# Four modulation chunks made into columns by TensorE, with x loaded first

## The reference, cut to what matters

```
c_act = silu(c)
mod = c_act @ w_ada + b_ada            # 1 x 6144: six vectors of 1024
sh_m, sc_m, g_m, sh_f, sc_f, g_f = split(mod, 6)
u = layer_norm(x) * (1 + sc_m) + sh_m  # mixer input
z = u @ w_in
```

## Time and profile before

| | us |
|---|---|
| median of 3 runs | 1428.12 (1427.02 to 1428.88) |
| the profiled execution, its own time | 1426.88 |
| its span in the profile | 1425.1 |
| TensorE busy in the span | 1393.0 |
| VectorE / ScalarE / GpSimd busy | 969.4 / 647.3 / 421.8 |

### The profile page before, as it was taken

How to read it: one execution, slowest core, us unless ns; L and a number is a source line. 1 busy time by engine, 2 the same in 40 slices (tenths; PEclk the granted TensorE clock), 3 DMA queues, 4 the chain that set the end, 5 groups by cost and what they waited for, 6 DMA issues and landing times.

```text
span 1425.1 us, 17299 instructions
## 1 busy us (share of the span) xinstructions
PE 1393.0 (98%) x6522; PEld 1148.6 (81%) x6522; DVE 969.4 (68%) x1340; ACT 647.3 (45%) x914; POOL 421.8 (30%) x453
## 2 busy tenths in 40 slices
PE   7799999999999999999999999999999999999996
PEld 3688888888888888888888888888888888888885
DVE  5789677776479946464768797556565646437787
ACT  5522677777542124101616774443345535343251
POOL 1006465555566000000024327333444200001315
PEclk9899999999999999999999999999999999999998
DMA  9775465654565232762622555444445878456361
GB/s 347 266 266 159 148 185 156 188 168 149 161 234 172 89 104 79 245 192 86 200 114 89 183 181 193 142 145 146 156 163 207 297 277 299 162 211 236 118 222 60
DMA packets 159083, 256.42 MB, mean 180 GB/s; under 512 B 11352, under 2 KB 81422, under 8 KB 159000
## 3 DMA queue, kind: packets, MB, share of 16 engines
q1 hardware_dynamic: 144152, 204.97, 43.1%
q0 software_dynamic: 14848, 50.34, 10.5%
HBM read 182.36 MB, written 68.71 MB: 176 GB/s over the span
## 4 chain that ended last, share of the span: by engine, by line
PE 91%; DVE 5%; ACT 2%; issue 1%; DMA 1%; SPq 0%; DVEq 0%; ACTq 0%
PE ps L2065 24%; PE ps L2067 24%; PE ps L2066 24%; PE ps L2214 11%; PE ps L2254 2%; PE ps L2264 2%; PE ps L2279 2%; PE ps L2085 1%; DVE part_lo L1922 1%; PE ps L2129 1%; PE ps L2404 1%; DVE q L1983 0%; DMA k_raw<-tw_scratch 0%; DMA ada<-in_w_ada_dram 0%; DVE w_lo L1387 0%
## 5 line engine op out<-in xcount | busy, mean ns | idle before, releaser
L2065 PE MATMUL ps<-act_hi,w_hi 128*128 128x512 f32 (+1 forms) x480 | 187.2, 390 | 9.4 <-DVE act_lo L1482 9.4
L1922 DVE TENSOR_TENSOR part_lo<-k_raw,part_hi 128x1024 fp32r<-128x1024 f32 x112 | 146.1, 1332 | 58.6 <-ACT part_hi L935 55.4
L2067 PE MATMUL ps<-act_hi,w_lo 128*128 128x512 f32 (+1 forms) x480 | 184.6, 385 | 0.0
L2066 PE MATMUL ps<-act_lo,w_hi 128*128 128x512 f32 (+1 forms) x480 | 184.6, 385 | 0.0
L2065 PE MATMUL ps<-part_hi 128*128 128x512 f32 x448 | 174.3, 389 | 0.0
L2066 PE MATMUL ps<-part_lo,part_hi 128*128 128x512 f32 x448 | 174.3, 389 | 0.0
L2067 PE MATMUL ps<-part_hi,part_lo 128*128 128x512 f32 x448 | 174.3, 389 | 0.0
L935 ACT ACTIVATE part_hi<-k_raw 128x1024 fp32r<-128x1024 f32 x112 | 116.4, 1059 | 113.6 <-DMA k_raw<-tw_scratch 48.8
L2065 PEld LDWEIGHTS ps<-act_hi,w_hi 128*128 128x128 f32 x480 | 91.1, 190 | 28.4 <-issue 5.9
L1387 DVE TENSOR_TENSOR w_lo<-w_raw,w_hi 128x1024 fp32r<-128x1024 f32 x51 | 65.9, 1291 | 65.6 <-ACT w_hi L935 65.6
L2066 PEld LDWEIGHTS ps<-act_lo,w_hi 128*128 128x128 f32 x480 | 91.2, 190 | 18.4 <-issue 1.0
(11 more groups left out here) (260 smaller groups left out, 3202.4 us busy)
## 6 DMA issues: line engine op xcount, KB each, us to landing
k_raw<-h_scratch SPq DMA_DIRECT2D x112, 256.0 KB, 4.2
w_raw<-in_w_in_dram SPq DMA_DIRECT2D x42, 512.0 KB, 4.1
ada<-in_w_ada_dram SPq DMA_DIRECT2D x8, 2048.0 KB, 9.6
tw_rows<-in_w_ff_dram POOLq DMA_DIRECT2D x64, 256.0 KB, 4.1
tw_scratch<-tw_sum POOLq DMA_DIRECT2D x32, 512.0 KB, 3.7
h_scratch<-h_sum POOLq DMA_DIRECT2D x64, 256.0 KB, 3.0
k_raw<-tw_scratch SPq DMA_DIRECT2D x64, 256.0 KB, 5.4
pair_raw<-in_w_ff_dram SPq DMA_DIRECT2D x13, 1024.0 KB, 6.3
```

Source lines behind the costliest of these rows:

```text
L1922: nc.vector.tensor_tensor(part_lo[s][:, :, :], k_raw[rs][:, :, :], f(part_hi[s][:, :, :]), ALU.subtract)\
L2065: nc.tensor.matmul(out, sh, mh, start=first, stop=False)
L2066: nc.tensor.matmul(out, sh, ml, start=False, stop=False)
L2067: return nc.tensor.matmul(out, sl, mh, start=False, stop=last)
```

## The change

x is read first, all eight tiles, then chunks 0 and 2, w_in blocks 0 and 1, chunks 1 and 3. All four mixer chunks take a new path, `direct_chunk`: a 128x128 block of the chunk is the stationary operand and c_act's single column moves past it, so that the result is a column at once. A half (four of the groups k) is 16 products, and both halves are summed by VectorE in `mixer_columns`. The row path and VectorE's work on chunks 1 and 3 go. On TensorE six transposes come first, then chunk 0 and 2 among the last two; chunks 1 and 3 are cut into eight pieces of 8 products, put between the parts of the lower stage. ScalarE's and VectorE's head loops are re-ordered tile by tile, and VectorE copies two tiles into `x_t` in place of one. Loads 3 to 6 of w_ada now wait for the chunk that held the buffer.

```diff
-N_DIRECT = 2
-ROW_ORDER = (0, 2, 1, 3)
-ADA_BANKS = {0: 0, 2: 1}
+N_DIRECT = 4
+DIRECT_ORDER = (0, 2, 1, 3)
...
             def load_ada(i):
-                if i == 3:
-                    sp.wait_ge(head_ps_done, 1)
...
+                if 3 <= i < 7:
+                    sp.wait_ge(reduced, DIRECT_ORDER.index(i - 3) + 1)
...
-            load_ada_half(0, 0)
-            load_x(range(2))
-            load_ada_half(0, 1)
-            load_x(range(2, 4))
+            load_x(range(ST))
+            load_ada(0)
...
-            load_ada_half(2, 0)
-            load_x(range(4, 6))
-            load_ada_half(2, 1)
-            load_x(range(6, ST))
+            load_ada(2)
             load_block(0)
+            load_block(1)
             load_ada(1)
-            load_block(1)
             load_ada(3)
...
-            for i in range(0, ST, 2):
...
+            for i in range(ST):
                 take_root(i, i)
+                if i >= 1:
+                    norm(i - 1, i - 1, mid[:, i - 1, :])
+                if i >= 2:
+                    save_tile(i - 2)
+            cut_hi(0)
...
+            for t in range(ST):
+                dve.wait_ge(x_in[t], 16)
+                stats(mid[:, t, :], t)
+                if t >= 1:
+                    scale_bias(t - 1, t - 1)
+            scale_bias(ST - 1, ST - 1)
...
-                link(nc.vector.tensor_tensor(out, total, bias, ALU.add))
+                link(nc.vector.tensor_tensor(out, low, bias, ALU.add))
+                link(nc.vector.tensor_tensor(out, high, out, ALU.add))
...
+            for t in (ST - 2, ST - 1):
+                dve.wait_ge(z_done, t + 1)
+                dve.wait_ge(x_copied, ST - 2)
+                nc.vector.tensor_copy(x_t[:, :, t * P:(t + 1) * P], tile_banks(t)).then_inc(x_copied, 1)
...
-            start_chunk(1)
             cut_u_lo(3)
-            end_chunk(1)
             cut_lo(2)
-            ada_chunk(3)
             mixer_columns(1)
...
+            def direct_chunk(i, half, ms=range(4)):
+
+                pe.wait_ge((ada_in, ada_end_in)[half][i % 3], 16 * (i // 3 + 1))
+                if i in (1, 3):
                     pe.wait_ge(cols_done, 1)
+                for m in ms:
+                    for k in range(4 * half, 4 * half + 4):
+                        ins = nc.tensor.matmul(ps[:, 6 + i % 2, 16 * half + 4 * i + m:16 * half + 4 * i + m + 1],
+                                               ada[i % 3][:, k, m * P:(m + 1) * P], c_act[:, k:k + 1],
+                                               start=k % 4 == 0, stop=k % 4 == 3)
+                if half == 1 and ms[-1] == 3:
+                    ins.then_inc(reduced, 1)
...
+            for i in range(6):
+                transpose_x(i)
             pe.wait_ge(head_sb_done, 2)
...
+            direct_chunk(0, 0)
+            transpose_x(6)
+            direct_chunk(0, 1)
+            transpose_x(7)
...
+            direct_chunk(2, 0)
+            direct_chunk(2, 1)
...
+            left, right = range(2), range(2, 4)
             pe.wait_ge(w_lo_done, 1)
             for k in range(2):
                 rows_part(0, k)
             pe.wait_ge(w_lo_done, 2)
             for k in range(2):
                 rows_part(1, k)
+                direct_chunk(1, 0, (left, right)[k])
             for n in range(2):
                 for k in range(2, 4):
                     rows_part(n, k)
+                    if n == 0:
+                        direct_chunk(1, 1, (left, right)[k - 2])
             pe.wait_ge(w_lo_done, 3)
             for k in range(4):
                 rows_part(2, k)
-            row_columns(1)
-            row_columns(3)
+                direct_chunk(3, k // 2, (left, right)[k % 2])
```

More of the change, by code:

```diff
@@ L125, in trunk_layer @@
     h_pad = at("h_pad", [P, 2, PAD + SEQ], f32, X + 84 * KB)
-    ada_row = [h_pad[0:1, i // 2, PAD + i % 2 * HALF:PAD + (i % 2 + 1) * HALF] for i in range(4)]
     z_pool = mid[:, 0:2, :]
@@ L356, in tile_banks @@
             return banks(2 + 2 * (i % 2)).rearrange("p (k s) -> p k s", s=P)
-        def partial_of(i):
-            return partial[0 if i == 3 else i % 4]
         SMALL_ROWS, SMALL_BIASES, SMALL_POOL = 16 * 8, 16 * 11, 16 * 15
@@ L960, in _ @@
             nc.scalar.activation(c_sig[:, :], c_raw[:, :], ACT.Sigmoid).then_inc(head_sb_done, 1)
-            def save_ada_row(i):
-                act.wait_ge(head_ps_done, {0: 1, 2: 4}[i])
-                copy(ada_row[i], ps[0:1, ADA_BANKS[i], :]).then_inc(head_sb_done, 1)
             def save_tile(i):
@@ L1430, in start_chunk @@
                 dve.wait_ge(ada_in[i % 3], 16 * (i // 3 + 1))
-                if i == 4:
-                    dve.wait_ge(reduced, 4)
-                elif i >= 8:
+                if i >= 8:
                     dve.wait_ge(reduced, i - 3)
-                link(nc.vector.tensor_scalar(partial_of(i)[:, :], ada[i % 3][:, 0, :], c_act[:, 0:1], None, ALU.mult))
+                link(nc.vector.tensor_scalar(partial[i % 4][:, :], ada[i % 3][:, 0, :], c_act[:, 0:1], None, ALU.mult))
                 add_rows(i, range(1, 4))
             def end_chunk(i):
-                if i in (1, 3):
-                    dve.wait_ge(ada_end_in[i % 3], 16 * (i // 3 + 1))
                 add_rows(i, range(4, 8))
             def add_rows(i, ks):
-                dst, src = partial_of(i)[:, :], ada[i % 3]
+                dst, src = partial[i % 4][:, :], ada[i % 3]
                 for k in ks:
@@ L1469, in mixer_columns @@
                 ks = slice(4 * h, 4 * h + 4)
-                out, total, bias = (t.rearrange("p (g k) -> p g k", g=2)[:, :, ks]
-                                    for t in (mod[:, 0:16], ps[:, 6 + h, 0:16], cols[:, 0:16]))
-                link(nc.vector.tensor_tensor(out, total, bias, ALU.add))
+                out, low, high, bias = (t.rearrange("p (g k) -> p g k", g=2)[:, :, ks] for t in (
+                    mod[:, 0:16], ps[:, 6 + h, 0:16], ps[:, 6 + h, 16:32], cols[:, 0:16]))
+                link(nc.vector.tensor_tensor(out, low, bias, ALU.add))
+                link(nc.vector.tensor_tensor(out, high, out, ALU.add))
                 scale = mod[:, KT + 4 * h:KT + 4 * h + 4]
@@ L1483, in cut_u_lo @@
                     .then_inc(u_lo_done, 1)
+            for t in (ST - 2, ST - 1):
+                dve.wait_ge(z_done, t + 1)
+                dve.wait_ge(x_copied, ST - 2)
+                nc.vector.tensor_copy(x_t[:, :, t * P:(t + 1) * P], tile_banks(t)).then_inc(x_copied, 1)
+            dve.wait_ge(head_ps_done, 2)
+            nc.vector.tensor_copy(cols[:, 0:ROWS_A], ps[:, 7, PIECE:PIECE + ROWS_A])
+            nc.vector.tensor_copy(cols[:, ROWS_A:ROWS_A + ROWS_C], ps[:, 7, PIECE + P:PIECE + P + ROWS_C])\
+                .then_inc(cols_done, 1)
             mixer_columns(0)
-            dve.wait_ge(z_done, ST)
-            nc.vector.tensor_copy(x_t[:, :, (ST - 1) * P:ST * P], tile_banks(ST - 1)).then_inc(x_copied, 1)
             cut_lo(0)
@@ L2079, in _ @@
             pe.wait_ge(consts_done, 2)
[L2081 to L2093, removed]
-                    pe.wait_ge(cols_done, 1)
[L2095 to L2102, removed]
+            def direct_chunk(i, half, ms=range(4)):
+                pe.wait_ge((ada_in, ada_end_in)[half][i % 3], 16 * (i // 3 + 1))
+                if i in (1, 3):
+                    pe.wait_ge(cols_done, 1)
+                for m in ms:
[5 more added lines that the diff above has]
+                    ins.then_inc(reduced, 1)
             def reduce_chunk(i):
```

## The result

The changed kernel takes 1456.46 us (1455.25 to 1457.42, 4 runs) against 1428.11 for before: the ratio is 1.0199, with a 95% interval of 1.0181 to 1.0216. It is slower by 28.4 us. I forecast 1448.7 and a range of 1440 to 1469.

The account below looks back on a forecast made before the run. TensorE, 98% busy, was taken as the bound, so a later upper stage moves the end. Columns at 43.2, lower stage from 47.4 to 80.9, upper stage at 85.2: 20.6 us later, median 1448.7, range 1440 to 1469.

Parts of the forecast that it names:

- the shift of the upper stage: Start of TensorE's upper stage: forecast at 85.2 instead of 64.58 us, 20.6 us later, all carried to the end.
- my forecast's own range: Whole kernel: 1444 to 1453 us, from columns at 41.4 to 45 and 3.4 us idle; 0.50 together with VectorE's relief.
- the first rival: Head: clock stays low, a record costs 0.235 us, columns come at 59.5, time 1465.0 us; chance 0.35.
- My own sign of being wrong: Whole kernel: records spaced 0.05 us, column-product loads running under the parts, or a granted clock of 0.50 after 25 us.
- The pieces and the lower stage: Lower stage: twelve parts 16.3 us, slow start 2.0, eight uncovered pieces 15.2; sum 33.5, from 47.4 to 80.9 us.
- the slow start of the first parts: Start of the lower stage: the first ten or so products run at 1.2 GHz, costing 2.0 us.
- The x tiles and the transposes: Head: first x tile lands at 5.7 us, ScalarE sets 2.35 us a tile, sixth transpose ends at 23.6.
- The price of a record in the head: Chunks 0 and 2 in the head: 0.119 us a record at 2.4 GHz, 128 records 15.2 us.
- The argument I used against it: Against a low clock in the head: it stayed at 1.00 across column products and into the gap from 60.43 us.
- Cheaper records: Column products: overlapping loads make records cheaper, break-even at 0.045 us; at 0.03 the median is 1424.3; chance 0.10.
- VectorE's relief: Behind the upper stage's start: relief pays back at most 3.4 us, best 1445.3; chance 0.50 together with the forecast.
- low clock did not hold in the mixed stage: Fourth rival, lower stage: low clock through alternating parts and column products adds up to 30 us, near 1495; 0.05 with others.

Follow-up runs that it names:

- The same program: The kernel before, its order kept, with column products instead of row products for chunks 0 and 2: median 1434.37 us, profiled runs 1442.08 and 1433.72 us.

## Why the prediction was right and where it was off

**Direction and range: right, the range with luck.** TensorE was the bound, its added work had no cover, and the shift of the upper stage (20.6 forecast, 28.8 measured) went to the end unchanged. But the loss was 28.4 us where I had added up 20.6. The measured 1456.46 lies outside my forecast's own range of 1444 to 1453 and outside the 1458 to 1468 of the first rival; the stated range held it because it covered both. My own sign of being wrong, a granted clock of 0.50 after 25 us, did appear.

**The pieces and the lower stage: right.** Forecast 33.5 us from the first part to the last piece, measured 33.3 (55.76 to 89.04). The record between parts was 0.105 and not 0.119, with 0.1 us of slow restart on the part behind it, so the piece was 1.8 and not 1.9; the slow start of the first parts cost 2.6 us and not 2.0, and the two errors nearly cancel. The lower price stood in my own rows: the chain has 1.69 us for the same sixteen records, 0.106 each, where I had taken the time of the loads. With VectorE in their place the time fell by 12.5 us; the terms of the sum give 12.7 (15.2 for the pieces, less 1.9 for the two `row_columns` and 0.56 of waiting).

**The x tiles and the transposes: right, a little early.** The first tile's statistics start at 5.04 (5.7 forecast), the pace is 1.9 to 2.0 us a tile on VectorE and 2.13 on ScalarE (2.35 forecast), the transposes of the sixth tile end at 21.87 (23.6).

**The price of a record in the head: wrong.** This is the term that failed, "128 records are 15.2 us" with at most 2.5 us for a slow start. They took 25.7 us (5.34 + 6.62 + 13.76), and the last transposes, the small ones included, took 4.1 instead of 2.6; against the 43.2 that I took, the columns came 8.5 us later, and nearly the whole miss of 8.2 us at the upper stage lies there. I took the price from a row of the right form, but that row stands right behind dense products; I let it hold for a long stretch of its own kind. The first rival, the low clock in the head, named the mechanism and had it at 0.35. It put the columns at 59.5 and the time at 1465.0; measured are 51.7 and 1456.46. It was too dark by half: 0.215 instead of 0.235 a record (2.6 us), the transposes 1.8 instead of 2.0, the sixth one 2.7 earlier, and the clock was high for part of the first half. The measured time lies between my forecast and this rival, and the runs show the rival's mechanism: row products in the same places give 10.7 us back, and a solid stretch of column products falls to 1.2 GHz behind dense work and without a pause.

**The argument I used against it was no evidence.** That the clock "stayed at 1.00 across the column products" rested on a 2.06 us stretch behind dense work; 24.61 us of the same show the fall.

**The other rivals.** Cheaper records did not occur: 0.105 at 2.4 GHz is above the 0.045 of break-even. VectorE's relief paid back nothing, TensorE's idle time behind the start being 3.6 us against 3.4. The low clock did not hold in the mixed stage.

**The page's rule on transposes.** The Trainium skill, "TensorE: Matmul & The Clock Gate", Part 4: PE-mode transpose, says that a transpose does not count as busy time that brings the full clock. The trace disagrees. Timeline rows of TensorE in the changed kernel, which had done nothing else until then:

```profile
10.07 3.37 PE L2086 MATMUL ps<-ident,mid 128*128 128x128 f32 x16 [10.07 <-ACT mid L940]
14.34 1.09 PE L2086 MATMUL ps<-ident,mid 128*128 128x128 f32 x8 [0.90 <-ACT mid L940]
```

The first tile took 1.95 us, the third 1.09: by the price the clock rose at about 12.9. The same kernel shows it in the clock column too, once that column counts: 0.50 from 16.3 to 19.7 and 1.00 behind it, while TensorE had still run nothing but transposes. By their prices all six kernels with x first rose in the first way, between about 12.9 and 16.3 us.

## What to carry to other kernels

Take the price of an instruction from a stretch that resembles the one it will stand in, its neighbours included: the same record cost 0.105 us among dense products and 0.215 among its own kind. Before work is moved from an engine with slack to the bound engine, ask what covers it; here 11.9 us of hidden VectorE work became 12.5 us of time. When a gap of the bound engine is filled, follow the next dependency: filling gaps alone gained nothing that can be told in two kernels, and 5.0 us once the columns behind it were also asked for earlier.

## What was not expected of the hardware

- A product with a 128x128 float32 stationary block and one moving column keeps TensorE busy by the record, yet a stretch of 24.6 us of them dropped the granted clock from 1.00 to 0.50 within the first 4 us, without a pause.
- The same program ran at 1431 and at 1442 us, by how much of its head of column products and transposes fell at 2.4 GHz.
- Transposes alone brought the clock up at the start, by their prices in the six kernels with x first, and once more at 19.7 us by the clock column of the changed kernel.
- The profile's clock column reads 1.00 until the first fall, also over the slow start: in the run at 1442.08 us the mean is given as 0.995, though 41 us of the head ran at the low level's price.
